# Filter network moved from the gate and up loop into the first down projection, buffers at multiples of 128 bytes, one weight ring instead of two

## The chip, the core and the metric

The kernel runs on one core of a Trainium2 chip. The metric is the device time of one execution in microseconds. A core has TensorE (PE, with its weight loads shown apart as PEld), VectorE (DVE), ScalarE (ACT), GpSimd (POOL) and SyncE (SP, which here only issues DMAs). Each has a queue of its own, worked off in order, and they meet at semaphores.

## The reference

One layer of an encoder trunk on x of 512 positions by 1024 channels, in float32:

```
x = x + 1/2 * SwiGLU_1(RMSNorm(x))            # 1024 -> 2816 -> 1024
h = RMSNorm(x); p = h @ W_in                  # -> q | k | v | x0 | x1 | v, 512 each
a = differential attention (4 heads, relative bias)
y = Hyena: short conv of width 3, long two-sided convolution, gates
x = x + concat([a, y]) @ W_out
x = x + 1/2 * SwiGLU_2(RMSNorm(x))
final RMSNorm
```

The long convolution's filters come from a small network on a position code z of 512 rows and 33 columns, which depends on no activation:

```
a = sin(freq * (z @ w1 + b1))                 # 33 -> 64
a = sin(freq * (a @ w2 + b2))                 # 64 -> 64
a = sin(freq * (a @ w3 + b3))                 # 64 -> 64
h = (a @ w4) * decay                          # 64 -> 2 x 512
```

## The kernel before

Activations lie with channels on the partitions and the 512 positions along the free axis, so each matmul is 128 x 128 weights against 128 x 512 activations. For float32 accuracy every operand is split into a high part (float32r) and the rest: each product of blocks is three matmuls, high by high, high by low, low by high (lines 1147, 1148, 1149).

Weights come in tiles of up to 8 blocks (0.5 MB), numbered through the kernel: 44 for gate and up of the first feed-forward layer (`N_FF1`), 24 for its down projection (`N_DOWN1`, in three chunks of 8, 8 and 6 blocks for each of 8 output blocks), 24 for the input projection (`N_MIX`), 8 for the output projection, and 44 and 24 again. For each tile SP loads it into one of four `raw` slots (line 282), waiting until the tile four before it has been split; ACT casts it to the high part (line 455), waiting until PE has used the tile two before it; DVE subtracts (line 723); PE runs 24 (or 18) matmuls. High and low parts have two halves in turn, in `w_hi` and `w_lo`, or for the down projection in `down_hi` and `down_lo`, which share their place with the DFT tables:

```
def ring(n):
    n = n if n < N_FF2 else n - N_FF2
    return (down_hi, down_lo) if N_DOWN1 < n <= N_MIX else (w_hi, w_lo)
```

In a pass of `gate_up` PE does a gate tile and an up tile, twice; DVE scales both sums by `rinv` (lines 810, 815), ACT takes Silu (line 498), DVE multiplies (line 820), ACT and DVE split the product into `h_hi` and `h_lo` (lines 502, 823). In a block j of `down` PE sums 22 blocks into bank 4 or 5, DVE adds half of it to the residual (`resid_add`, line 738), ACT squares it and makes `x_hi` (`resid_block`, lines 462 and 464), DVE makes `x_lo` (line 758). PE goes on to the next block in the other bank meanwhile.

The filter network is laid into passes 1 to 4 of the first gate and up loop. `mlp(k)` on PE (line 1195) is one float32 matmul, shown as two; `mlp_argument(k)` on DVE adds the bias, multiplies by the frequency and brings the argument into the range of Sin in seven instructions (lines 769 to 787); `mlp_sin(k)` on ACT takes Sin (line 474). PE's `mlp(k)` waits for `mlp_sin(k - 1)`. The result `act3` is read by the filters' matmuls at the start of the mixer stage (line 1312). The four DFT tables (0.5 MB each) are loaded by SP behind the sixth load of the input projection (lines 310 to 314).

`place` gives a buffer the next multiple of 32 bytes. The base and most sizes are multiples of 128; `rinv`, `ssq` and `lam_in` start 32 bytes past one, and `x0c`, `vx`, `vx_nat` and `q_hi` 96 bytes past one.

Of the kernel before, what the change touches and what calls it, by code (L numbers as in the profile page):

```python
# [14 lines left out]
P = 128  # L15
# [19 lines left out]
SPLIT = 2  # L35

# [39 lines left out]
def build(nc, a, out):  # L76
    ctx = ExitStack()
    with ctx:
# [5 lines left out]
        base = (nc.sbuf_base - SLAB * 4 + 31) // 32 * 32  # L84
# [23 lines left out]
        lam_in, _ = place("lam_in", [P, 4, DK])  # L108
# [5 lines left out]
        k_hi, _ = place("k_hi", [P, S], F32R)  # L114

        act3, _ = place("act3", [FO, S])
# [4 lines left out]
        cos_t, tables_at = place("cos_t", [P, NT, FQ])  # L121
        sin_t, _ = place("sin_t", [P, NT, FQ])
        cos_i, _ = place("cos_i", [P, 2, S])
        sin_i, _ = place("sin_i", [P, 2, S])
# [49 lines left out]
        z_t, _ = place("z_t", [EMB, S], at=late_at)  # L174
        w1, _ = place("w1", [EMB, FO], at=late_at + 4 * S)
        w2, _ = place("w2", [FO, FO], at=late_at + 4 * (S + FO))
        act_a, _ = place("act_a", [FO, 2, S], at=late_at + 4 * 2 * S)
        w3, _ = place("w3", [FO, FO], at=late_at + 4 * 4 * S)
# [77 lines left out]
        def ring(n):  # L256

            n = n if n < N_FF2 else n - N_FF2
            return (down_hi, down_lo) if N_DOWN1 < n <= N_MIX else (w_hi, w_lo)

# [14 lines left out]
        def _(sp):  # L275
# [8 lines left out]
            def others():  # L284

                sp.dma_start(z_t[:], a["c_z"]).then_inc(mlp_landed, 16)
                sp.dma_start(w1[:], a["hy_f_w1"][0]).then_inc(mlp_landed, 16)
                with nc.allow_non_contiguous_dma(reason="columns of constants"):
                    for k, name in enumerate(("hy_f_b1", "hy_f_b2", "hy_f_b3", "hy_f_freq")):
                        sp.dma_start(mlp_c[:, k:k + 1], a[name].rearrange("o f -> f o")).then_inc(mlp_landed, 16)  # L290
                    sp.dma_start(w2[:], a["hy_f_w2"][0]).then_inc(mlp_landed, 16)
                    sp.dma_start(w3[:], a["hy_f_w3"][0]).then_inc(mlp_landed, 16)
# [60 lines left out]
            gate_up(a["ffn1_w_gate"][0], a["ffn1_w_up"][0], N_FF1)  # L353
            down(a["ffn1_w_down"][0], N_DOWN1)
            w = a["w_in"][0].rearrange("(k p) f -> p k f", p=P)
            for h in range(HEADS):
                for m in range(6):
                    load(w[:, :, m * D_ATT + h * P:m * D_ATT + (h + 1) * P], KD, N_MIX + 6 * h + m)
                if h == 0:
                    dft_tables()  # L360
# [84 lines left out]
        def _(act):  # L445
# [5 lines left out]
            def split(kb, n0, stride=0, i=0):  # L451
                slot, half = n0 % RAW, n0 % SPLIT
                act.wait_ge(raw_landed[slot], number(16 * (n0 // RAW + 1), 16 * stride // RAW, i))
                wait(act, w_used, number(n0 - SPLIT + 1, stride, i))
                nc.scalar.copy(ring(n0)[0][:, half, 0:kb, :], raw[:, slot, 0:kb, :]).then_inc(w_hi_made, 1)  # L455
# [16 lines left out]
            def mlp_sin(k):  # L472
                act.wait_ge(mlp_arg, k + 1)
                nc.scalar.activation(act3[:] if k == 2 else act_a[:, k, :], mlp_u[:], ACT.Sin).then_inc(mlp_act, 1)


            def gate_up(ffn, n_first, i, first=False, other=None):
                for b in range(2):
# [6 lines left out]
                    if other and b == 0:  # L485
                        other()
# [17 lines left out]
            def down(s, i, last=False):  # L504
# [204 lines left out]
        def _(dve):  # L709
# [9 lines left out]
            def split(kb, n0, stride=0, i=0):  # L719
                slot, half = n0 % RAW, n0 % SPLIT  # L720
                dve.wait_ge(w_hi_made, number(n0 + 1, stride, i))
                hi, lo = ring(n0)
                nc.vector.tensor_tensor(lo[:, half, 0:kb, :], raw[:, slot, 0:kb, :],  # L723
                                        hi[:, half, 0:kb, :].bitcast(F32), ALU.subtract).then_inc(w_split, 1)
# [66 lines left out]
            def gate_up(ffn, n_first, i, first=False, other=()):  # L791

                other = list(other) + [lambda: None] * 4
                for b in range(2):
# [18 lines left out]
                    other[2 * b]()  # L813
# [11 lines left out]
                    other[2 * b + 1]()  # L825

            def down(s, i, last=False):
# [26 lines left out]
            for i in range(4):  # L854
                gate_up(0, N_FF1, i, first=i == 0, other=mlp_argument(i - 1) if i else ())
# [10 lines left out]
            with dve.Fori(0, 2) as i:  # L866
                down(1, i)
# [269 lines left out]
        def _(pe):  # L1137

            def tile(dst, operand, n0, stride=0, i=0, first=True, last=True, ready=None, between=None):
# [3 lines left out]
                hi_w, lo_w = ring(number(n0, stride, i) if isinstance(i, int) else n0)  # L1143
                for k, (hi, lo) in enumerate(operand):
                    if ready:
                        pe.wait_ge(ready[0], ready[1] + k + 1)
                    nc.tensor.matmul(dst, hi_w[:, half, k, :], hi, start=first and k == 0, stop=False)  # L1147
                    nc.tensor.matmul(dst, hi_w[:, half, k, :], lo, start=False, stop=False)  # L1148
                    ins = nc.tensor.matmul(dst, lo_w[:, half, k, :], hi, start=False, stop=last and k == kb - 1)  # L1149
# [12 lines left out]
            def gate_up(ffn, n_first, i, first=False, other=None):  # L1162
                for b in range(2):
# [15 lines left out]
                    if other and b == 0:  # L1179
                        other()  # L1180

            def down(s, i, first=False):
                for j in range(4):
                    wait(pe, resid_set, number(KD * (s - 1) + j - 1, 4, i))
# [5 lines left out]
            def mlp(k):  # L1190
                src = (z_t[:], act_a[:, 0, :], act_a[:, 1, :])[k]
# [51 lines left out]
            for i in range(4):  # L1243
                gate_up(0, N_FF1, i, first=i == 0, other=(lambda: mlp(i - 1)) if i else None)
# [7 lines left out]
            down(1, 0, first=True)  # L1252
# [316 lines left out]
```

## Time and profile before

| | us |
|---|---|
| median of 3 runs | 1064.8 |
| lowest and highest | 1063.46 and 1067.45 |
| the profiled execution, its own time | 1066.42 |
| its span, first to last instruction | 1064.6 |
| PE busy | 1037.0 (97%) |
| DVE busy | 568.4 (53%) |
| ACT busy | 334.7 (31%) |
| POOL busy | 60.8 (6%) |
| a 0.5 MB load of gate or up weights, issue to landing, median | 3.7 |

The times of rows come from that one profiled execution and are counted from the start of its span. Busy time of PE overlaps: a matmul of 512 columns is shown as 0.39 us, and in the dense stream the next one starts 0.23 us after it. The mean granted clock of TensorE is 0.987 of full speed.

### The profile page before, as it was taken

To read this page: it belongs to the slowest core of one execution; us is meant where nothing else is said; L and a number is where in the kernel's file an instruction comes from. 1 tells how busy PE (TensorE), PEld (TensorE's weight loads), DVE (VectorE), ACT (ScalarE), POOL (GpSimd) and SP (SyncE) were. 2 spreads that over 40 slices of the span, in tenths; PEclk is the share of its full clock that TensorE was granted. 3 is DMA by queue.
4 is the path that set the end of the run, shared out by engine and by line. 5 is a ranking of instruction groups with operands and counts; after the bars stand their busy time and mean duration, and the time that the engine had idled before them with its cause. 6 is when DMAs were issued, how large, how long until landed. Compare 5 with 4: busy or idle time off the path is not lost. (4 is left out here: it accounts for less than half of the span.)

```text
span 1064.6 us, 12059 instructions
## 1 busy us (share of the span) xinstructions
PE 1037.0 (97%) x4551; PEld 821.8 (77%) x4551; DVE 568.4 (53%) x722; ACT 334.7 (31%) x477; POOL 60.8 (6%) x57
## 2 busy tenths in 40 slices
PE   8999999999999999999999969999999999999996
PEld 7777788888888876777775558878888888888885
DVE  5556554544333358686857595764444445433332
ACT  6222222222232233444444203442222222222222
POOL 0000000000000010000000070310000000000000
PEclk9999999999999998999999989999999999999999
DMA  7523323333333373222221000323333332332322
GB/s 220 95 84 94 99 83 100 93 99 94 100 98 91 92 242 90 76 80 80 77 79 40 1 20 20 91 88 99 99 99 99 95 100 82 96 105 90 94 70 79
DMA packets 184460, 96.69 MB, mean 91 GB/s; under 512 B 14811, under 2 KB 181859, under 8 KB 184424
## 3 DMA queue, kind: packets, MB, share of 16 engines
q1 hardware_dynamic: 183160, 92.70, 30.0%
q0 software_dynamic: 352, 1.85, 0.6%
q10 hardware_dynamic: 912, 1.64, 0.5%
q8 instruction: 24, 0.39, 0.2%
q14 instruction: 12, 0.10, 0.0%
HBM read 94.07 MB, written 2.11 MB: 90 GB/s over the span
## 5 line engine op out<-in xcount | busy, mean ns | idle before, releaser
L1147 PE MATMUL bank<-x_hi,w_hi 128*128 128x512 f32 x872 | 345.5, 396 | 3.3 <-DVE w_lo L723 2.9
L1149 PE MATMUL bank<-x_hi,w_lo 128*128 128x512 f32 x872 | 340.5, 391 | 0.0
L1148 PE MATMUL bank<-x_lo,w_hi 128*128 128x512 f32 x872 | 340.4, 390 | 0.0
L723 DVE TENSOR_TENSOR w_lo<-raw,w_hi 128x1024 fp32r<-128x1024 f32 x121 | 148.0, 1223 | 110.6 <-ACT w_hi L455 106.2
L1147 PEld LDWEIGHTS bank<-x_hi,w_hi 128*128 128x128 f32 x872 | 164.3, 188 | 49.9 <-issue 10.1
L1149 PEld LDWEIGHTS bank<-x_hi,w_lo 128*128 128x128 f32 x872 | 164.3, 188 | 34.7
L1148 PEld LDWEIGHTS bank<-x_lo,w_hi 128*128 128x128 f32 x872 | 164.4, 189 | 34.3 <-issue 1.0
L455 ACT CAST w_hi<-raw 128x1024 fp32r<-128x1024 f32 x121 | 126.6, 1046 | 52.3 <-PE bank L1451 32.1
L1147 PE MATMUL bank<-h_hi,down_hi 128*128 128x512 f32 x336 | 130.7, 389 | 0.0
L1148 PE MATMUL bank<-h_lo,down_hi 128*128 128x512 f32 x336 | 130.7, 389 | 0.0
L1149 PE MATMUL bank<-h_hi,down_lo 128*128 128x512 f32 x336 | 130.7, 389 | 0.0
L723 DVE TENSOR_TENSOR down_lo<-raw,down_hi 128x1024 fp32r<-128x1024 f32 (+1 forms) x47 | 55.5, 1182 | 110.5 <-ACT down_hi L455 110.2
L502 ACT CAST h_hi<-bank 128x512 f32 (+1 forms) x44 | 25.8, 587 | 207.5 <-DVE bank L820 207.5
L455 ACT CAST down_hi<-raw 128x1024 fp32r<-128x1024 f32 (+1 forms) x47 | 45.8, 974 | 112.2 <-PE bank L1149 112.2
L1148 PEld LDWEIGHTS bank<-h_lo,down_hi 128*128 128x128 f32 x336 | 63.1, 188 | 13.2
L1147 PEld LDWEIGHTS bank<-h_hi,down_hi 128*128 128x128 f32 x336 | 63.1, 188 | 13.0
L1149 PEld LDWEIGHTS bank<-h_hi,down_lo 128*128 128x128 f32 x336 | 63.1, 188 | 13.0
L395 POOL TENSOR_TENSOR ssq<-ssq,sq 128x512 f32<-128x512 f32 x24 | 32.4, 1352 | 651.0 <-ACT sq L462 650.7
L498 ACT ACTIVATE silu<-bank 128x512 f32<-128x512 f32 x44 | 26.3, 599 | 132.2 <-DVE bank L810 132.2
L815 DVE TENSOR_TENSOR bank<-bank,rinv 128x512 f32<-128x512 f32 x44 | 30.7, 699 | 67.9 <-PE bank L1149 67.8
L810 DVE TENSOR_TENSOR bank<-bank,rinv 128x512 f32<-128x512 f32 x44 | 30.7, 698 | 39.2 <-PE bank L1149 39.2
L823 DVE TENSOR_TENSOR h_lo<-bank,h_hi 128x512 f32 (+1 forms) x44 | 30.4, 691 | 36.0 <-ACT h_hi L502 36.0
(222 smaller groups left out, 866.6 us busy)
## 6 DMA issues: line engine op xcount, KB each, us to landing
raw<-in_ffn_w_gate SPq DMA_DIRECT2D x44, 512.0 KB, 3.7
raw<-in_ffn_w_up SPq DMA_DIRECT2D x44, 512.0 KB, 3.7
raw<-in_ffn_w_down SPq DMA_DIRECT2D x32, 512.0 KB, 3.4
raw<-in_w_in SPq DMA_DIRECT2D x24, 512.0 KB, 3.8
raw<-in_ffn_w_down SPq DMA_DIRECT2D x16, 384.0 KB, 3.0
raw<-in_w_out SPq DMA_DIRECT2D x8, 512.0 KB, 3.4
x_nat<-in_x SPq DMA_DIRECT2D x4, 512.0 KB, 7.0
out<-o_nat SPq DMA_DIRECT2D x8, 256.0 KB, 2.9
```

Of the source, the lines that this page charges most:

```text
L395: nc.gpsimd.tensor_tensor(ssq[:], ssq[:], sq[:, b, :], ALU.add).then_inc(ssq_added, 1)
L455: nc.scalar.copy(ring(n0)[0][:, half, 0:kb, :], raw[:, slot, 0:kb, :]).then_inc(w_hi_made, 1)
L498: nc.scalar.activation(silu[:, b, :], bank[b][:], ACT.Silu).then_inc(gate_act, 1)
L502: nc.scalar.copy(h_hi[:, number(b, 2, i), :], bank[2 + b][:]).then_inc(h_hi_made, 1)
L723: nc.vector.tensor_tensor(lo[:, half, 0:kb, :], raw[:, slot, 0:kb, :], hi[:, half, 0:kb, :].bitcast(F32), ALU.subtract).then_inc(w_split, 1)
L810: nc.vector.tensor_tensor(bank[b][:], bank[b][:], rinv[:], ALU.mult).then_inc(gate_scaled, 1)
L815: nc.vector.tensor_tensor(bank[2 + b][:], bank[2 + b][:], rinv[:], ALU.mult).then_inc(up_scaled, 1)
L823: nc.vector.tensor_tensor(h_lo[:, at, :], bank[2 + b][:], h_hi[:, at, :].bitcast(F32), ALU.subtract).then_inc(h_split, 1)
L1147: nc.tensor.matmul(dst, hi_w[:, half, k, :], hi, start=first and k == 0, stop=False)
L1148: nc.tensor.matmul(dst, hi_w[:, half, k, :], lo, start=False, stop=False)
L1149: ins = nc.tensor.matmul(dst, lo_w[:, half, k, :], hi, start=False, stop=last and k == kb - 1)
```

## The change

The three steps of the filter network leave the gate and up loop and go into blocks 1, 2 and 3 of the first down projection: `mlp(j - 1)` ahead of block j on PE, the parts of `mlp_argument(j - 1)` behind the three splits of block j on DVE, and `mlp_sin(j - 1)` behind `resid_block(j)` on ACT. The loops of ACT and DVE over the down projection's halves become straight code, and ACT's loop over the gate passes begins at 1 instead of 5. Sin writes `act3` each time. The separate ring goes: all tiles use `w_hi` and `w_lo`, and the DFT tables have a place to themselves and are loaded with the small constants at the start. The network's input z lies in the place of `k_hi`, and its weights w1 to w3 in that of `lam_in`, loaded behind the first layer's gate and up weights. Buffers of 512 bytes and more begin at multiples of 128 bytes.

```diff
-                at = top[0]
-                top[0] += (size + 31) // 32 * 32
+                line = LINE if size >= 512 else 32
+                at = (top[0] + line - 1) // line * line
+                top[0] = at + size
...
-        down_lo, _ = place("down_lo", [P, SPLIT, 8, P], F32R, at=tables_at)
-        down_hi, _ = place("down_hi", [P, SPLIT, 8, P], F32R, at=tables_at + 4 * SPLIT * 8 * P)
...
+        z_t, _ = place("z_t", [EMB, S], at=k_hi_at)
+        w1, _ = place("w1", [EMB, FO], at=lam_in_at)
+        w2, _ = place("w2", [FO, FO], at=lam_in_at + 4 * FO)
+        w3, _ = place("w3", [FO, FO], at=lam_in_at + 8 * FO)
...
-            def dft_tables():
-
-                sp.wait_ge(w_used, N_MIX + 1)
                 sp.dma_start(cos_t[:], a["c_cos"].rearrange("(t p) f -> p t f", p=P)).then_inc(dft_landed, 16)
...
+            def mlp_weights():
+
+                sp.wait_ge(lam_dot, 2)
+                for dst, name in ((w1, "hy_f_w1"), (w2, "hy_f_w2"), (w3, "hy_f_w3")):
+                    sp.dma_start(dst[:], a[name][0]).then_inc(mlp_landed, 16)
...
             gate_up(a["ffn1_w_gate"][0], a["ffn1_w_up"][0], N_FF1)
+            mlp_weights()
             down(a["ffn1_w_down"][0], N_DOWN1)
...
+            def down(s, i, last=False, sines=False):
                 for j in range(4):
                     for c in range(3):
                         if not (last and j == 3 and c == 2):
                             split(CHUNKS[(c + 1) % 3][1], N_STAGE[s] + 3 * j + c + 1, 12, i)
                     resid_block(s, j, 4, i)
+                    if sines and j:
+                        mlp_sin(j - 1)
...
-            for i in range(5):
-                gate_up(0, N_FF1, i, first=i == 0, other=(lambda: mlp_sin(i - 2)) if i > 1 else None)
-            with act.Fori(5, NF // 2) as i:
+            gate_up(0, N_FF1, 0, first=True)
+            with act.Fori(1, NF // 2) as i:
                 gate_up(0, N_FF1, i)
             act.wait_ge(cols_landed, 16 * 10)
-            with act.Fori(0, 2) as i:
-                down(1, i)
+            down(1, 0, sines=True)
+            down(1, 1)
...
+            def down(s, i, last=False, arguments=False):
                 for j in range(4):
                     for c in range(3):
                         if not (last and j == 3 and c == 2):
                             split(CHUNKS[(c + 1) % 3][1], N_STAGE[s] + 3 * j + c + 1, 12, i)
+                        if arguments and j:
+                            for part in mlp_argument(j - 1)[(0, 1, 2)[c]:(1, 2, 4)[c]]:
+                                part()
                     resid_add(s, j, 4, i)
...
-            with dve.Fori(0, 2) as i:
-                down(1, i)
+            down(1, 0, arguments=True)
+            down(1, 1)
...
-                hi_w, lo_w = ring(number(n0, stride, i) if isinstance(i, int) else n0)
...
+            def down(s, i, first=False, mlps=False):
                 for j in range(4):
+                    if mlps and j:
+                        mlp(j - 1)
                     wait(pe, resid_set, number(KD * (s - 1) + j - 1, 4, i))
...
-                gate_up(0, N_FF1, i, first=i == 0, other=(lambda: mlp(i - 1)) if i else None)
+                gate_up(0, N_FF1, i, first=i == 0)
...
-            down(1, 0, first=True)
+            down(1, 0, first=True, mlps=True)
             down(1, 1)
```

## Rows read from the trace of the kernel before

**Rows 1.** Waits, 24 to 250 us: engine, line, releaser; total us, times, longest.
```profile
PE bank L1147 <- DVE w_lo L723: 2.9, 4, 0.9
```

**Rows 2.** Timeline of PE: start, length, line, operation; in brackets the idle time before.
```profile
45.93 0.39 PE L1149 MATMUL bank<-x_hi,w_lo 128*128 128x512 f32 x1
46.25 1.07 PE L1195 MATMUL bank<-z_t,w 33*64 33x512 f32 x2
47.25 0.50 PE L1147 MATMUL bank<-x_hi,w_hi 128*128 128x512 f32 x1
...
52.61 0.39 PE L1149 MATMUL bank<-x_hi,w_lo 128*128 128x512 f32 x1
53.92 0.50 PE L1147 MATMUL bank<-x_hi,w_hi 128*128 128x512 f32 x1 [0.93 <-DVE w_lo L723]
```

**Rows 3.** Timeline of all engines at the end of block 1 of the down projection.
```profile
289.33 1.22 DVE L723 TENSOR_TENSOR down_lo<-raw,down_hi 128x1024 fp32r<-128x1024 f32 x1 [4.69 <-ACT down_hi L455]
...
291.90 0.39 PE L1149 MATMUL bank<-h_hi,down_lo 128*128 128x512 f32 x1
...
292.45 0.69 DVE L738 SCALAR_TENSOR_TENSOR resid<-bank,resid 128x512 f32 x1 [1.89 <-PE bank L1149]
...
293.26 0.63 ACT L462 ACTIVATE sq<-resid 128x512 f32 x1 [3.97 <-DVE resid L738]
...
293.80 0.71 ACT L464 ACTIVATE x_hi<-resid,cols  x1
...
294.41 1.04 ACT L455 CAST down_hi<-raw 128x1024 fp32r<-128x1024 f32 x1
```

**Rows 4.** ACT: a Sin on the timeline, and the group of Silu's table loads.
```profile
62.97 0.63 ACT L474 ACTIVATE act_a<-mlp_u 64x512 f32<-64x512 f32 x1
```
```profile
L498 ACT ACT_TABLE_LOAD x2 | 2.6, 1283 | 0.0
```

**Rows 5.** Timeline of DVE: last parts of an argument.
```profile
57.22 1.39 DVE L769 SCALAR_TENSOR_TENSOR mlp_u<-mlp_k,mlp_u 64x512 f32<-64x512 f32 x2
...
62.53 0.41 DVE L787 TENSOR_SCALAR mlp_u<-mlp_u 64x512 f32<-64x512 f32 x1
```

**Rows 6.** PE's timeline, its chain, and stretches (length, busy, granted clock, DMA share, GB/s).
```profile
393.75 5.71 PE L1312 MATMUL bank<-w,act 64*128 64x512 f32 x12
...
402.77 0.79 PE L1147 MATMUL bank<-x_hi,w_hi 128*128 128x512 f32 x1
```
```profile
616.12 0.39 PE L1451 MATMUL bank<-ma_hi,w_lo 128*128 128x512 f32 x1
```
```profile
650.67 3.51 PE bank L1342 x32
...
655.66 0.43 PE bank L1449
```
```profile
401.00:402.00 1.00, 1.00 (x3) 0.69 1.20 291
...
408.00:409.00 1.00, 1.00 (x5) 0.90 0.00 0
```
```profile
619.80:619.90 0.10, 0.00 (x0) 0.63 0.00 0
```
```profile
654.00:655.00 1.00, 1.00 (x4) 0.50 1.03 363
```

**Rows 7.** SP's and ACT's timelines, and a stretch with the tables' DMAs (last: GB/s).
```profile
41.58 0.41 SPq L282 DMA_DIRECT2D raw<-in_ffn_w_gate  x1
```
```profile
55.00 1.04 ACT L455 CAST w_hi<-raw 128x1024 fp32r<-128x1024 f32 x1
```
```profile
396.00:398.00 2.00, 1.99 (x5) 1.00 1.10 363
```

**Rows 8.** Groups by line and shape: shapes, count, busy us, mean ns, idle before.
```profile
L820 DVE TENSOR_TENSOR bank<-bank,silu 128x512 f32<-128x512 f32 x44 | 30.8, 700 | 4.5
L815 DVE TENSOR_TENSOR bank<-bank,rinv 128x512 f32<-128x512 f32 x44 | 30.7, 699 | 67.9 <-PE bank L1149 67.8
```

More of the change, by code:

```diff
@@ L35 @@
 SPLIT = 2
+LINE = 128
 N_FF1 = 0
@@ L83, in build @@
         slab = ctx.enter_context(nc.sbuf_tensor("slab", [P, SLAB], F32))
-        base = (nc.sbuf_base - SLAB * 4 + 31) // 32 * 32
+        base = (nc.sbuf_base - SLAB * 4 + 127) // 128 * 128
         top = [base]
@@ L107, in build @@
         ssq, _ = place("ssq", [P, S])
-        lam_in, _ = place("lam_in", [P, 4, DK])
+        lam_in, lam_in_at = place("lam_in", [P, 4, DK])
         lam, _ = place("lam", [P, 8])
@@ L113, in build @@
         mlp_c, _ = place("mlp_c", [FO, 4])
-        k_hi, _ = place("k_hi", [P, S], F32R)
+        k_hi, k_hi_at = place("k_hi", [P, S], F32R)
+        cos_t, _ = place("cos_t", [P, NT, FQ])
+        sin_t, _ = place("sin_t", [P, NT, FQ])
+        cos_i, _ = place("cos_i", [P, 2, S])
+        sin_i, _ = place("sin_i", [P, 2, S])
         act3, _ = place("act3", [FO, S])
@@ L173, in build @@
         late_at = hid_at + 4 * (2 * NF - 7) * S
[L174 to L178, printed above, removed]
+        z_t, _ = place("z_t", [EMB, S], at=k_hi_at)
+        w1, _ = place("w1", [EMB, FO], at=lam_in_at)
+        w2, _ = place("w2", [FO, FO], at=lam_in_at + 4 * FO)
+        w3, _ = place("w3", [FO, FO], at=lam_in_at + 8 * FO)
         rel, _ = place("rel", [BUCKETS, HEADS], at=late_at + 4 * (4 * S + FO))
@@ L254, in number @@
             return n0 + i * stride if stride else n0
-        def ring(n):
-            n = n if n < N_FF2 else n - N_FF2
-            return (down_hi, down_lo) if N_DOWN1 < n <= N_MIX else (w_hi, w_lo)
         def col(name, k=0):
@@ L454, in split @@
                 wait(act, w_used, number(n0 - SPLIT + 1, stride, i))
-                nc.scalar.copy(ring(n0)[0][:, half, 0:kb, :], raw[:, slot, 0:kb, :]).then_inc(w_hi_made, 1)
+                nc.scalar.copy(w_hi[:, half, 0:kb, :], raw[:, slot, 0:kb, :]).then_inc(w_hi_made, 1)
             def resid_block(s, j, stride=0, i=0):
@@ L473, in mlp_sin, with gate_up @@
                 act.wait_ge(mlp_arg, k + 1)
-                nc.scalar.activation(act3[:] if k == 2 else act_a[:, k, :], mlp_u[:], ACT.Sin).then_inc(mlp_act, 1)
-            def gate_up(ffn, n_first, i, first=False, other=None):
+                nc.scalar.activation(act3[:], mlp_u[:], ACT.Sin).then_inc(mlp_act, 1)
+            def gate_up(ffn, n_first, i, first=False):
                 for b in range(2):
@@ L484, in gate_up @@
                         split(8, n + 1, 4, i)
-                    if other and b == 0:
-                        other()
                     if head:
@@ L502, in gate_up @@
                     nc.scalar.copy(h_hi[:, number(b, 2, i), :], bank[2 + b][:]).then_inc(h_hi_made, 1)
-            def down(s, i, last=False):
+            def down(s, i, last=False, sines=False):
                 for j in range(4):
@@ L721, in split @@
                 dve.wait_ge(w_hi_made, number(n0 + 1, stride, i))
-                hi, lo = ring(n0)
-                nc.vector.tensor_tensor(lo[:, half, 0:kb, :], raw[:, slot, 0:kb, :],
-                                        hi[:, half, 0:kb, :].bitcast(F32), ALU.subtract).then_inc(w_split, 1)
+                nc.vector.tensor_tensor(w_lo[:, half, 0:kb, :], raw[:, slot, 0:kb, :],
+                                        w_hi[:, half, 0:kb, :].bitcast(F32), ALU.subtract).then_inc(w_split, 1)
             def resid_add(s, j, stride=0, i=0):
@@ L788, in mlp_argument, with gate_up @@
                 return argument, turns, rest, clamp
-            def gate_up(ffn, n_first, i, first=False, other=()):
-                other = list(other) + [lambda: None] * 4
+            def gate_up(ffn, n_first, i, first=False):
                 for b in range(2):
@@ L812, in gate_up @@
                         split(8, n + 2, 4, i)
-                    other[2 * b]()
                     dve.wait_ge(w_used, number(n + 2, 4, i))
@@ L824, in gate_up @@
                                             ALU.subtract).then_inc(h_split, 1)
-                    other[2 * b + 1]()
-            def down(s, i, last=False):
+            def down(s, i, last=False, arguments=False):
                 for j in range(4):
@@ L854, in _ @@
             for i in range(4):
-                gate_up(0, N_FF1, i, first=i == 0, other=mlp_argument(i - 1) if i else ())
+                gate_up(0, N_FF1, i, first=i == 0)
             for k in range(2):
@@ L1146, in tile @@
                         pe.wait_ge(ready[0], ready[1] + k + 1)
-                    nc.tensor.matmul(dst, hi_w[:, half, k, :], hi, start=first and k == 0, stop=False)
-                    nc.tensor.matmul(dst, hi_w[:, half, k, :], lo, start=False, stop=False)
-                    ins = nc.tensor.matmul(dst, lo_w[:, half, k, :], hi, start=False, stop=last and k == kb - 1)
+                    nc.tensor.matmul(dst, w_hi[:, half, k, :], hi, start=first and k == 0, stop=False)
+                    nc.tensor.matmul(dst, w_hi[:, half, k, :], lo, start=False, stop=False)
+                    ins = nc.tensor.matmul(dst, w_lo[:, half, k, :], hi, start=False, stop=last and k == kb - 1)
                     if between and k == kb // 2:
@@ L1160, in sum_squares, with gate_up @@
                 nc.tensor.matmul(bank[7][:], ones[:], ssq[:], start=True, stop=True).then_inc(ssq_summed, 1)
-            def gate_up(ffn, n_first, i, first=False, other=None):
+            def gate_up(ffn, n_first, i, first=False):
                 for b in range(2):
@@ L1178, in gate_up @@
                     tile(bank[2 + b][:], x_ops, n + 1, 4, i)
-                    if other and b == 0:
-                        other()
-            def down(s, i, first=False):
+            def down(s, i, first=False, mlps=False):
                 for j in range(4):
+                    if mlps and j:
+                        mlp(j - 1)
                     wait(pe, resid_set, number(KD * (s - 1) + j - 1, 4, i))
@@ L1190, in mlp @@
             def mlp(k):
-                src = (z_t[:], act_a[:, 0, :], act_a[:, 1, :])[k]
+                src = (z_t, act3, act3)[k][:]
                 if k == 0:
@@ L1243, in _ @@
             for i in range(4):
-                gate_up(0, N_FF1, i, first=i == 0, other=(lambda: mlp(i - 1)) if i else None)
+                gate_up(0, N_FF1, i, first=i == 0)
             pe.wait_ge(late_landed, 32)
```

9 lines of the change are left out of this document (removed).

## The prediction

> **What bounds the kernel now.** I read the list of waits for PE first, then the timelines of PE, DVE and ACT around the filter network, then the granted clock in one-microsecond stretches. PE is busy nearly the whole span, so only PE's time counts: an edit on ACT, DVE or a DMA queue has a price only where PE waits for it. In the first gate and up loop PE waits four times for a weight split, and nothing else [rows 1]. The reader should see where three of those four sit: behind the filter network. The dense stream starts a 128x512 matmul every 0.23 us; at 45.93 it is cut by mlp(0), and the stream's next start is at 47.25. A second hole follows one tile later, 52.61 to 53.92, with 0.93 us of it put down to w_lo [rows 2].
>
> **The change part by part.**
>
> *Filter network out of the gate loop.* Two costs go, three times each. The network's matmul takes 47.25 - 45.93 - 0.23 = 1.09 us from the stream, and the hole at the next tile 53.92 - 52.61 - 0.23 = 1.08 us [rows 2]. That hole is DVE's: its argument waits for mlp's matmul, the up scaling queues behind it, then silu product, h_hi and h_lo, and only then the split of the next weights. In both places the first matmul after the hole takes 0.50 us instead of 0.39 [rows 2], 0.1 us more each. That is 1.09 + 1.08 + 0.2 = 2.4 us an iteration, in three iterations **-7.2 us**.
>
> *Filter network into the first down projection.* mlp(0) stands before block j = 1 and needs only z_t and w1, loaded long before: its own 1.09 + 0.1 = 1.2 us, no wait. mlp(1) and mlp(2) are different. PE issues mlp(1) before block 2, and it waits for Sin(0); ACT issues Sin(0) behind resid_block(1), which waits for resid_add(1), which waits for the last matmul of block 1. So PE has to see block 1 end, and then wait for a chain that today lies under block 2. The rows of such a block [rows 3] give its length. With T = 291.90 the start of the block's last matmul: resid_add starts at T+0.55, the square at T+1.36, x_hi at T+1.90, and the next ACT instruction at T+2.51 (today a weight cast; in the change Sin). Sin took 0.63 us [rows 4], so act3 is there at T+3.14 and mlp(1) starts at about T+3.2. Its two passes last 1.0 us (46.25 to 47.25, rows 2) and the stream resumes near T+4.2 with the 0.1 us slow start, against T+0.23 today: 4.1 us, of which 2.9 are an idle PE. Behind PE's wait stand mlp(1) and all of block 2. Two such waits (the third Sin is awaited by nobody until the filters): 8.2. Together **+9.4 us**.
>
> Does the argument chain come later still? In the last tile of a block DVE has from 290.55 (289.33 + 1.22) to 292.45 free [rows 3], 1.90 us. Into it go two of the subtractions, 1.39 us, and the clamp, 0.41 [rows 5]. With the short waits between them it just fits; at worst resid_add comes some 0.1 us later. I take nothing. ACT's and DVE's next weight splits run during PE's stall and are not late.
>
> *Table set for Sin.* Silu's set is loaded twice in the whole kernel, once for each feed-forward layer, although Sin ran three times between Silus [rows 4]: no load was needed, and Square and Copy did not evict it either. Bounds: 0 and one load of 1.28 us. I take 0.
> The Trainium skill (ScalarE: Activation LUTs, "What ACT_TABLE_LOAD costs") prices a switch of sets at about 2.7 us, drain included. By it a switch ahead of Sin(0) would add 2.7 us once, an estimate from that page; the rows show no switch.
>
> *The clock.* A stall of 2.9 us and then 1.0 us of matmuls on 64 rows and 64 columns is 3.9 us without dense work. What did the granted clock do after such stretches? After a matmul that ended at 616.51 (616.12 + 0.39) PE idled, and the clock fell from 2.4 to 1.2 GHz at about 619.8, 3.3 us on; it also fell at 654.0, after 3.3 us of 2-column matmuls that had begun at 650.67 and kept PE busy [rows 6]. Mine is as long or longer, with a little more work in it than either, so I expect a fall at each of the two stalls. The price at the lower clock: matmuls start every 0.43 us, not 0.23 (655.66 lasts 0.43 on the chain, rows 6). After 654.0 eight matmuls ran so, 8 x 0.20 = 1.6 us. During the filters it fell at about 401.4 and rose at about 408.2, and from 402.77 on that is some 13 to 14 dense matmuls, 14 x 0.20 = 2.8 us [rows 6]. Bounds for each stall: 0 and 2.8; I take 1.6, because dense work follows at once, as it did at 654. Two: **+3.2 us**.
> The Trainium skill (TensorE: Matmul & The Clock Gate, Part 1, "What's actually happening") has half clock as the default and activity as what lifts it, so by it a stall in a dense stage costs more than its own length. This speaks against the change, and the trace agrees. Without it the sum would be +2.2 us, with it +5.4.
>
> *DFT tables moved to the start.* Four DMAs of 0.5 MB go onto SP's queue before the load of weight tile 8, and three small ones leave it. They pass no wait there. Tile 8's load was issued at 41.58; its cast began at 55.00, and would begin 2.4 us earlier without mlp(0), at 52.6 [rows 7]. When these tables moved in the mixer stage the engines carried 363 GB/s, other loads among it [rows 7], so 2.1 MB take 6 to 7 us; and with the 3.7 us that such a load takes to land (median, page) tile 8 is there at about 41.6 + 6.5 + 3.7 = 52, just at its cast; PE comes to tile 8 only two tiles' splits later, past 56. Cover: the four raw slots. If the cover goes, PE waits us for us. Bounds 0 and 3 us; I take 0. In the mixer stage the DMAs go away, but no PE wait there is for a DMA, and DVE sets the pace: 0. The three weight loads behind the gate loads wait for the lambda sums, which DVE has done before its gate loop begins, and pass SP's down loads by three issues, with four raw slots as cover: 0.
>
> *128-byte starts, one ring.* Of what PE streams in its big groups, everything already starts at multiples of 128 bytes by the order of the placements; rinv and ssq do not (32 past), nor do the last mixer buffers. DVE's product with rinv took 699 ns, and with silu, which is aligned, 700 [rows 8]: 0. The down ring had two halves like w_hi and w_lo and the same waits, so one ring waits no longer: 0. ACT's and DVE's loops that become straight code are off the path: 0.
>
> **Sum.** -7.2 + 9.4 + 3.2 = +5.4 us. The profiled execution took 1066.4 us with a span of 1064.6, 1.6 above the median of the three runs shown, 1064.8, which themselves span 4 us. Against that median: 1070.2 us.
>
> **The rivals.**
> - *Both stalls, both followed by the lower clock*, 1070.2, up to 1072.6 with 2.8 us at each: 0.45. For it: the chain is in the order of the queues, and the clock fell in less.
> - *Only one of them followed by it*, +3.8 to +5.0: 1068.6 to 1069.8; 0.20. For it: a stretch of 3.9 us is little longer than the 3.3 us after which it fell, so where the stall meets the clock may decide.
> - *The clock holds*: +2.2, 1067.0; 0.17. For it: PE idles 2.9 us, less than the 3.3 after which it fell at 619.8. Against it: the stretch of two-column matmuls. It decides where the granted clock stays 1.00 in the down stage.
> - *A table load before Sin(0)*: +1.3 on top, 1071.5; 0.06. Rows 4 speak against it.
> - *Tile 8 late*: if the tables move at half the rate above, it lands some 4 to 5 us later than I say, and PE stands 3 us at about 57 us: 1073; 0.04.
> - *The other side, the mixer's start gets faster without the tables' traffic*: the 16 filter matmuls took from 393.75 to 402.77 [rows 6], 9.0 us where 16 x 0.5 = 8.0 would do, and the clock was low after them. Were that gone, up to 1 us and the 2.8 of low clock come back; with the clock held in the down stage too that is 2.2 - 3.8 = -1.6, 1063.2. It decides only if DVE's chain of filters starts earlier, and that chain shows no DMA wait: 0.05.
> The rest, 0.03, is for what I don't see.
>
> **How the numbers follow.** The point is the first case. About 0.5% (5.3 us) is what a measurement of this kernel can tell from no change. Slower than that, above 1070.1: the first case, the table load, the late tile, less some of their lower edge: 0.51. Within: one fall, clock holds, the eased mixer, and the edge: 0.44. Faster: 0.05. The range leaves out the tails of the last rivals: 1066.0 to 1073.2, which holds the clock-holds case at its low end and two long falls at its upper; the first case alone is 1069.6 to 1072.9.
>
> **What would show it.** In the profile after: no PE wait for w_lo in iterations 1 to 3 beyond the first short one, and iterations of 21.8 us; an idle PE of about 2.9 us ahead of the second and third mlp matmul, put down to ACT's Sin, near 286 and 305 us (block 1 ends at 291.9 - 7.2 + 1.2); granted clock 0.5 after each; no new ACT_TABLE_LOAD; tile 8's cast not waiting for a DMA; the tables' four DMAs near 40 us. Wrong would be: a stall of another length (then the chain of rows 3 is not the chain), a clock at 1.00 after it, or any shift in the mixer's or the second layer's stages, where I expect none.

## The result, and the profile after

| | before | after |
|---|---|---|
| median, us | 1064.13 (4 runs, 1062.98 to 1067.45) | 1077.15 (4 runs, 1076.40 to 1079.40) |
| ratio to before | | 1.0121, 95% interval 1.0093 to 1.0149 |
| the profiled execution, its time and span | 1066.42, 1064.6 | 1077.56, 1075.8 |
| mean granted clock of that execution | 0.987 | 0.985 |

The change costs 13.0 us in the medians, 11.2 us between the two profiled spans. 1070.2 was predicted, with a range up to 1073.2: slower, as forecast, but outside the range.

First the list of waits of PE, 24 to 400 us, in the kernel after (engine, line, releaser; total us, times, longest). It answers to [rows 1].

```profile
PE bank L1184 <- ACT act L466: 5.2, 2, 2.6
PE bank L1136 <- DVE w_lo L713: 0.3, 1, 0.3
```

The waits for w_lo behind the filter network are gone; in their place stand two for Sin, 2.6 us each (the stalls, below). The timeline after, around the second network matmul `mlp(1)` (start, length, engine, line; idle time before in brackets; rows between are left out), answers to [rows 3]:

```profile
286.22 0.39 PE L1138 MATMUL bank<-h_hi,w_lo 128*128 128x512 f32 x1
286.26 0.42 DVE L777 TENSOR_SCALAR mlp_u<-mlp_u 64x512 f32<-64x512 f32 x1
286.64 0.69 DVE L728 SCALAR_TENSOR_TENSOR resid<-bank,resid 128x512 f32<-128x512 f32 x1
287.37 0.63 ACT L454 ACTIVATE sq<-resid 128x512 f32<-128x512 f32 x1 [3.79 <-DVE resid L728]
287.90 0.71 ACT L456 ACTIVATE x_hi<-resid,cols 128x512 fp32r<-128x512 f32 x1
...
288.52 0.61 ACT L466 ACTIVATE act<-mlp_u 64x512 f32<-64x512 f32 x1
...
289.19 1.96 PE L1184 MATMUL bank<-act,w 64*64 64x512 f32 x2 [2.58 <-ACT act L466]
...
311.51 1.07 PE L1184 MATMUL bank<-act,w 64*64 64x512 f32 x2 [2.58 <-ACT act L466]
```

That is the predicted chain, link by link: last matmul of block 1, resid_add, square, x_hi, Sin, and only then PE; the last row is `mlp(2)`, with the same wait. The clamp ends at 286.68 and resid_add begins at 286.64: the argument just fits, as the prediction had it. What came behind the wait, in one-microsecond stretches (length, then busy time of PE, PEld, DVE, ACT and POOL, granted clock, DMA share, GB/s):

```profile
289.00:290.00 1.00, 0.81 (x1) 0.28 (x2) 0.97 (x1) 1.00 (x2) 0.42 (x1) 0.61 0.00 0
290.00:291.00 1.00, 1.00 (x2) 0.00 (x0) 0.90 (x1) 0.07 (x1) 0.00 (x0) 0.50 0.00 0
295.00:296.00 1.00, 1.00 (x4) 0.72 (x3) 0.00 (x0) 0.00 (x0) 0.00 (x0) 0.50 0.00 0
296.00:297.00 1.00, 1.00 (x6) 0.82 (x5) 0.00 (x0) 0.00 (x0) 0.00 (x0) 0.98 0.00 0
313.00:314.00 1.00, 1.00 (x5) 0.77 (x4) 1.00 (x2) 0.00 (x0) 0.00 (x0) 0.55 0.00 0
314.00:315.00 1.00, 1.00 (x4) 0.81 (x3) 0.78 (x2) 0.00 (x0) 0.00 (x0) 0.50 0.07 23
316.00:317.00 1.00, 1.00 (x5) 0.80 (x4) 0.00 (x0) 0.00 (x0) 0.00 (x0) 0.74 0.27 80
```

TensorE went from 2.4 to 1.2 GHz at both stalls. After the first it stayed there from 289.2 to 296.0, the whole `mlp(1)` (1.96 us instead of 1.07) and some eleven dense matmuls; after the second, where `mlp(2)` had still run at full rate from 311.51, from 313.1 to 316.5, some eight dense matmuls.

None of this explains the size. To find the rest, take the same instruction in both traces (of DVE, and for the output projection of PE), kernel after minus kernel before, along the whole span:

| start of the instruction | after minus before, us |
|---|---|
| the gate loop's beginning, end of passes 1, 2, 3, end of the loop | -0.4, -2.8, -5.2, -7.7, -7.7 |
| resid_add of blocks 0, 1, 2, 3 of the first down projection | -7.4, -5.8, +1.6, +7.3 |
| of blocks 4, 5, 6, 7 | +7.7, +8.1, +8.4, +8.8 |
| first `q_t` of the mixer stage, second `q_t` and later | +9.0, +7.0 |
| output projection, PE on `mh_hi`: first matmul, last | +6.9, +7.6 |
| last instruction of the second layer's gate loop | +7.6 |
| resid_add of blocks 0 to 7 of the second down projection | +8.1, 8.5, 9.0, 9.4, 9.8, 10.3, 10.7, 11.2 |

The steps at blocks 2 and 3 are the stalls. The last row has nothing of the filter network in it, and yet each block is 0.44 us longer. So something runs slower throughout the down projections, and in the output projection too. On the timeline of PE, kernel after, in the second down projection, where PE waits for nothing:

```profile
1014.88 0.39 PE L1137 MATMUL bank<-h_lo,w_hi 128*128 128x512 f32 x1
1015.11 0.40 PE L1138 MATMUL bank<-h_hi,w_lo 128*128 128x512 f32 x1
1015.34 0.39 PE L1136 MATMUL bank<-h_hi,w_hi 128*128 128x512 f32 x1
1015.57 0.40 PE L1137 MATMUL bank<-h_lo,w_hi 128*128 128x512 f32 x1
1015.81 0.39 PE L1138 MATMUL bank<-h_hi,w_lo 128*128 128x512 f32 x1
1016.04 0.40 PE L1136 MATMUL bank<-h_hi,w_hi 128*128 128x512 f32 x1
```

and in the kernel before:

```profile
1000.09 0.39 PE L1147 MATMUL bank<-h_hi,down_hi 128*128 128x512 f32 x1
1000.32 0.39 PE L1148 MATMUL bank<-h_lo,down_hi 128*128 128x512 f32 x1
1000.55 0.39 PE L1149 MATMUL bank<-h_hi,down_lo 128*128 128x512 f32 x1
1000.77 0.39 PE L1147 MATMUL bank<-h_hi,down_hi 128*128 128x512 f32 x1
```

From one `h_hi,w_hi` to the next, a *triple* of matmuls, it takes 0.70 us after (1015.34 to 1016.04) and 0.68 before (1000.09 to 1000.77). Over all recorded pairs of neighbours in the second down projection (175 in each kernel) the means are 0.700 and 0.680. The two layers have 2 x 176 such triples: 352 x 0.02 = 7.0 us. In the gate loops and the input projection the triple is 0.68 in both kernels. In the output projection it is not: where PE streams `mh_hi` and `mh_lo`, which lie in h's place by then, it is 0.70 after and 0.68 before, and its part of the same loss is 0.7 us:

```profile
696.73 0.39 PE L1438 MATMUL bank<-mh_hi,w_hi 128*128 128x512 f32 x1
...
697.43 0.40 PE L1438 MATMUL bank<-mh_hi,w_hi 128*128 128x512 f32 x1
```

```profile
687.08 0.39 PE L1449 MATMUL bank<-mh_hi,w_hi 128*128 128x512 f32 x1
...
687.76 0.39 PE L1449 MATMUL bank<-mh_hi,w_hi 128*128 128x512 f32 x1
```

In the two stretches of the down projection the clock is 1.00, the instructions and their order are the same, and PE waits for nothing. A row's own length (0.39 or 0.40) hardly shows it; only starts, three apart, do.

### The profile page after: what moved, and what is told of

Its sections match the earlier page's. It is cut to its first block and busy times, and to the rows that moved or that the text cites. A ratio compares the mean times of both kernels' runs of the same rounds, so it can differ in the third digit from the quotient of the medians.

```text
span 1075.8 us, 11999 instructions
## 1 busy us (share of the span) xinstructions
PE 1045.6 (97%) x4551; PEld 823.2 (77%) x4551; DVE 570.3 (53%) x722; ACT 335.0 (31%) x477; POOL 60.7 (6%) x57
## 5 line engine op out<-in xcount | busy, mean ns | idle before, releaser
L713 DVE TENSOR_TENSOR w_lo<-raw,w_hi 128x1024 fp32r<-128x1024 f32 x168 | 203.7, 1213 | 236.6 <-ACT w_hi L447 232.0
L447 ACT CAST w_hi<-raw 128x1024 fp32r<-128x1024 f32 x168 | 172.3, 1026 | 183.8 <-PE bank L1138 146.5
L1136 PE MATMUL bank<-h_hi,w_hi 128*128 128x512 f32 x352 | 141.0, 400 | 0.0
L1137 PE MATMUL bank<-h_lo,w_hi 128*128 128x512 f32 x352 | 140.4, 399 | 0.0
L1138 PE MATMUL bank<-h_hi,w_lo 128*128 128x512 f32 x352 | 140.4, 399 | 0.0
L1136 PEld LDWEIGHTS bank<-h_hi,w_hi 128*128 128x128 f32 x352 | 67.1, 191 | 19.2 <-issue 3.2
L1138 PEld LDWEIGHTS bank<-h_hi,w_lo 128*128 128x128 f32 x352 | 67.1, 191 | 16.2
L1137 PEld LDWEIGHTS bank<-h_lo,w_hi 128*128 128x128 f32 x352 | 67.2, 191 | 16.0
L454 ACT ACTIVATE sq<-resid 128x512 f32<-128x512 f32 x24 | 15.1, 630 | 78.4 <-DVE resid L728 66.8
L808 DVE TENSOR_TENSOR bank<-bank,silu 128x512 f32<-128x512 f32 x44 | 30.8, 700 | 4.5
```

The lines of the kernel that those rows point to most:

```text
L447: nc.scalar.copy(w_hi[:, half, 0:kb, :], raw[:, slot, 0:kb, :]).then_inc(w_hi_made, 1)
L713: nc.vector.tensor_tensor(w_lo[:, half, 0:kb, :], raw[:, slot, 0:kb, :], w_hi[:, half, 0:kb, :].bitcast(F32), ALU.subtract).then_inc(w_spl ...
L808: nc.vector.tensor_tensor(bank[2 + b][:], bank[2 + b][:], silu[:, b, :], ALU.mult).then_inc(h_made, 1)
L1136: nc.tensor.matmul(dst, w_hi[:, half, k, :], hi, start=first and k == 0, stop=False)
L1137: nc.tensor.matmul(dst, w_hi[:, half, k, :], lo, start=False, stop=False)
L1138: ins = nc.tensor.matmul(dst, w_lo[:, half, k, :], hi, start=False, stop=last and k == kb - 1)
```

## The experiments

What differs between the two dense streams is where the operands lie. `place` in the change moves `h_hi` from byte 138624 to 138752 of a partition and `h_lo` from 183680 to 183808. The first of each pair is 128 past a multiple of 256, the second is on one. `w_hi` (82048) and `w_lo` (90240) lie 128 past a multiple of 256 in both kernels, and so do `x_hi` and `x_lo`, and `down_hi` and `down_lo` in the kernel before. So my theory became: the stream is slow when the activations and the weights start at different places modulo 256. Its rivals: the single ring, `h` on a multiple of 256 by itself, the DFT tables' new place, or something of the profile alone. "Past" below always means past a multiple of 256 bytes.

### h_plus128: the kernel after, h moved by 128 bytes

```diff
+        top[0] += 128
         hid_at = top[0]
```

> The changed kernel with h_hi and h_lo 128 bytes further on (138880 and 183936 instead of 138752 and 183808), nothing else. In the changed kernel three matmuls of one block take 0.70 us in both down projections, 0.68 in every other stage. Placement theory (the start of h decides the rate of the stream): 0.68 in both down projections, 16 blocks x 0.43 = 6.9 us less than the changed kernel, about 1070 us. Ring theory (down weights in w_hi and w_lo cost the time): 0.70 stays, about 1077.

Measured: 1071.39 us (7 runs, 1068.04 to 1071.65) beside 1064.94 of before (16 runs), ratio 1.0047, interval 1.0031 to 1.0064; the kernel after stood at 1.0121. One line of placement gives back 5.8 us in the medians, 6.6 with each median taken against the kernel before of its own series. The same stretch of PE's timeline:

```profile
1015.04 0.39 PE L1137 MATMUL bank<-h_hi,w_hi 128*128 128x512 f32 x1
...
1015.73 0.39 PE L1137 MATMUL bank<-h_hi,w_hi 128*128 128x512 f32 x1
...
1016.40 0.39 PE L1137 MATMUL bank<-h_hi,w_hi 128*128 128x512 f32 x1
```

A triple is 0.68 again (1.36 for two). The end of the second down projection, 11.15 us behind before in the kernel after, is 2.7 us behind here. Both waits for Sin are as in the kernel after; the clock fell only at the second:

```profile
289.53 1.07 PE L1185 MATMUL bank<-act,w 64*64 64x512 f32 x2 [2.60 <-ACT act L467]
290.53 0.50 PE L1137 MATMUL bank<-h_hi,w_hi 128*128 128x512 f32 x1
...
308.38 1.55 PE L1185 MATMUL bank<-act,w 64*64 64x512 f32 x2 [2.60 <-ACT act L467]
```

```profile
290.00:291.00 1.00, 1.00 (x4) 0.43 (x3) 0.87 (x2) 0.42 (x1) 0.00 (x0) 1.00 0.00 0
309.00:310.00 1.00, 1.00 (x3) 0.14 (x1) 0.95 (x2) 0.26 (x1) 0.00 (x0) 0.50 0.00 0
```

This run prices the parts of a stall apart. Without a fall a stall costs 3.9 us (resid_add stands at -5.44 in block 1 and -1.55 in block 2 against before), with one 5.5 (-1.55 to +3.93).

### before_one_ring: the kernel before, its second ring gone

```diff
-            n = n if n < N_FF2 else n - N_FF2
-            return (down_hi, down_lo) if N_DOWN1 < n <= N_MIX else (w_hi, w_lo)
+            return (w_hi, w_lo)
```

> The kernel before with all weight tiles in w_hi and w_lo; the down ring's place stays unused, every address stays. Ring theory: 0.70 us for three matmuls in both down projections, about 1071. Placement theory: 0.68, within 1 us of the kernel before, about 1064.

Measured: 1065.87 us (10 runs), ratio 1.0001, interval 0.9988 to 1.0014; triple 0.680. The single ring costs nothing that this measurement can tell from 0, and is not what slows the stream.

### before_h_plus128: the kernel before, h moved by 128 bytes

```diff
+        top[0] += 128
         hid_at = top[0]
```

> The kernel before, down ring kept, with h_hi and h_lo (and the mixer buffers that share their place) 128 bytes further on, at 138752 and 183808 as in the changed kernel. Placement theory: 0.70 us for three matmuls in both down projections, about 1071. Ring theory: 0.68, about 1064.

Measured: 1073.75 us (4 runs), ratio 1.0074, interval 1.0047 to 1.0100; the triple in both down projections 0.700. The same line that mends the kernel after harms the kernel before, since here it takes h from 128 past to 0 past. Two rings, the old place of the tables, the filter network in the gate loop: none of that prevents it. The mixer's buffers in h's place move along, and `mh_hi`'s triple is 0.697 here too. The predicted 352 x 0.02 = 7.0 us lies in the interval of 5.0 to 10.7 us.

### w_plus384: the kernel after, the weights moved instead

```diff
         raw, _ = place("raw", [P, RAW, 8, P])
+        cols, _ = place("cols", [P, NCOLS])
+        top[0] = (top[0] + 127) // 128 * 128
         w_hi, _ = place("w_hi", [P, SPLIT, 8, P], F32R)
```

(`cols` leaves its old place.) Weights are now 0 past, like h; x stays 128 past.

> The changed kernel with cols placed ahead of w_hi, so that w_hi and w_lo start 384 bytes further on, at 0 past a multiple of 256 where they were 128 past one; x_hi, x_lo and h stay. If the start of h alone counts: down 0.70, gate and up 0.68, about 1077. If it is the pair of activations and weights: down 0.68 (both at 0 past 256) and gate, up and input projection 0.70 (x is 128 past, weights 0): 110 tiles x 24 x 0.0065 = 17 us more and 7 less, about 1087. Ring theory: as the changed kernel.

Measured: 1083.82 us (4 runs), ratio 1.0165, interval 1.0145 to 1.0185. The down triple is 0.680 with h still 0 past, and the gate, up and input projection's triple has become 0.70 (0.697 to 0.700 by stage). So it is neither h's place nor the weights' alone, but the two together: what one edit mends in the down projections, it breaks in the larger part of the kernel. The time is 3 us under the 1087 that was expected. Part of that is in the trace: the output projection, left out of the sum, gains 0.7 us here (0.70 back to 0.68), and the first gate loop and the input projection stayed at 0.697 and 0.698.

### w32_h64, w64_h128, w96_h192: other distances

Single executions, for the stream's rate alone, on before_one_ring: the weights start 32, 64 or 96 bytes further on, h twice as far, x stays. One of the three, the others alike:

```diff
+        top[0] += 64
         w_hi, _ = place("w_hi", [P, SPLIT, 8, P], F32R)
...
+        top[0] += 64
         hid_at = top[0]
```

> before_one_ring with weights 32 bytes and h 64 bytes further on: x starts 32 bytes less than w, h 32 bytes more, counted modulo 256. If only equality modulo 256 is fast: 0.70 us for three matmuls everywhere. If a difference below 128 costs nothing: 0.68 everywhere. If the cost grows with the distance: between, or less than 0.68 somewhere.

> before_one_ring with weights 64 bytes and h 128 bytes further on: x starts 64 bytes less than w, h 64 bytes more, modulo 256. Same alternatives: 0.70 everywhere (only equality is fast), 0.68 everywhere (a difference below 128 costs nothing), or between.

> before_one_ring with weights 96 bytes and h 192 bytes further on: x starts 96 bytes less than w, h 96 bytes more, modulo 256. From the two such runs before: 0.70 us where x stands below w by 32 and 64, 0.70 and 0.687 where h stands above by 32 and 64. Only equality is fast: about 0.70 for both. No theory has less than 0.68.

Measured: 1090.96, 1084.10 and 1091.15 us. The mean triple by the distance (activations minus weights, modulo 256), from these runs and those above:

| distance | triple, us | run and stream |
|---|---|---|
| 0 | 0.680 | kernel before, gate and down; w_plus384, down |
| +128 | 0.700 | kernel after, down; w_plus384, gate |
| -32, +32 | 0.700, 0.700 | w32_h64, gate and down |
| -64, +64 | 0.700, 0.687 | w64_h128, gate and down |
| -96, +96 | 0.703, 0.700 | w96_h192, gate and down |

Only equal starts gave 0.680. None of the distances of 32, 64 and 96 bytes is as good. Each of them was measured with one pair of starts only, so the table doesn't show that the distance alone decides; for 0 (both at 128, both at 0) and for 128 (0 against 128, either way round) there are two.

### h_lo_plus128 and w_lo_plus384: one operand of the pair

```diff
         h_hi, _ = place("h_hi", [P, NF, S], F32R)
+        top[0] += 128
         h_lo, _ = place("h_lo", [P, NF, S], F32R)
```

> The changed kernel with only h_lo 128 bytes on: h_hi starts at 0, h_lo at 128 past a multiple of 256, both weights at 128. If each matmul pays for its own pair of activations and the weights that lie in or go into the array with it: high by low (the one that streams h_lo) starts the next one after 0.227 us, the other two after 0.233; three take 0.693. If one bad operand spoils all three: 0.70; if the pair is decided by the high parts: 0.70; by the low parts: 0.68.

> The changed kernel with cols ahead of w_lo, so that w_lo starts at 0 past a multiple of 256 and w_hi stays at 128; x at 128, h at 0. While x_lo or h_lo streams, the array loads w_lo for the next matmul; while the two others stream it loads w_hi. If the weights that are loaded during the stream count: in the down stage high by low is fast (0.227) and the others slow, three in 0.693; in the gate loop high by low is slow, three in 0.687. If the weights already in the array count: the same sums, but the fast one of down and the slow one of the gate loop is the matmul with w_lo itself.

(The second puts `cols` ahead of `w_lo` alone.) If each matmul had its own price by its own pair of operands, the down triple of h_lo_plus128 (two matmuls of three unequal) would be 0.693, and in w_lo_plus384 the gate triple (one of three) 0.687 and the down triple (two of three) 0.693. Measured: 0.687, and 0.693 and 0.700; the times were 1077.16 and 1088.35 us. That simple form of the theory is refuted. A price set by neighbours too (which weights load while which activations stream) would be a candidate; no run separates it, and what the hardware does inside stays open. That all four equal is fast, and anything else measured is slower, stands.

### net_in_gate: placement, ring and tables of the change, without moving the network

The kernel before with one ring, the new `place`, the DFT tables in a place of their own and loaded at the start, and h 128 past; `mlp`, its arguments and Sin stay in the gate loop.

```diff
-                at = top[0]
-                top[0] += (size + 31) // 32 * 32
+                line = LINE if size >= 512 else 32
+                at = (top[0] + line - 1) // line * line
+                top[0] = at + size
...
+        top[0] += 128
         hid_at = top[0]
...
-                if h == 0:
-                    dft_tables()
```

> The whole change but the filter network's move, with h 128 bytes on: one ring, 128-byte starts, DFT tables loaded at the start; the network stays in the gate loop. If tables, ring and the other starts cost and give nothing: the kernel before, 1065 within 2 us. If the early tables delay weight tile 8 or ease the mixer stage: up to 3 us more or 4 us less.

Measured: 1065.81 us (10 runs) beside 1066.25 of before (19 runs), ratio 0.9991, interval 0.9974 to 1.0007. PE's wait for w_lo is that of [rows 1], four times, 2.9 us in all. The prediction's zeros for the ring, the tables and the other starts hold within this interval, as long as h stays 128 past.

### sin_early: the kernel after, mended

With h as in h_plus128, Sin goes ahead of the residual's square and x_hi on ACT, and the parts of the argument into the block's first two tiles on DVE:

```diff
-                    resid_block(s, j, 4, i)
                     if sines and j:
                         mlp_sin(j - 1)
+                    resid_block(s, j, 4, i)
...
-                            for part in mlp_argument(j - 1)[(0, 1, 2)[c]:(1, 2, 4)[c]]:
+                            for part in mlp_argument(j - 1)[(0, 2, 4)[c]:(2, 4, 4)[c]]:
```

> h_plus128 with Sin(j-1) issued ahead of resid_block(j) instead of behind it, and DVE's argument done in the first two tiles of a block instead of all three. Theory of the step (PE waits for the chain resid_add, square, x_hi, Sin, 2.6 us twice, and one of two stalls brought the lower clock): no wait of mlp for ACT, granted clock 1.00 in the down stage, so h_plus128 less 2 x 2.9 and less some 1.6: about 1061 us, 3.6 below the kernel before (three matmuls of the network at 1.2 us stay, three holes at 1.2 us go). Rival (the stall has another cause, such as the network's place in the stage): the waits stay, about 1068.

Measured: 1061.54 us (10 runs, 1059.39 to 1064.48) beside 1066.25 of before (19 runs), ratio 0.9966, interval 0.9951 to 0.9982. It beats both kernels. PE's timeline where the first stall was:

```profile
286.01 0.39 PE L1139 MATMUL bank<-h_hi,w_lo 128*128 128x512 f32 x1
...
286.33 1.07 PE L1185 MATMUL bank<-act,w 64*64 64x512 f32 x2
...
287.33 0.50 PE L1137 MATMUL bank<-h_hi,w_hi 128*128 128x512 f32 x1
```

```profile
287.00:288.00 1.00, 1.00 (x4) 0.59 (x4) 0.13 (x1) 0.84 (x2) 0.05 (x1) 1.00 0.82 246
```

No wait, no fall, and a step of 1.2 us at each `mlp` (resid_add at -7.2, -6.0, -4.8, -3.5 in blocks 0 to 3): moving the network is worth 7.2 - 3 x 1.2 = 3.6 us if nobody waits. The network's small matmuls are still there, so they alone did not bring the lower clock; in these runs it fell there only where the wait stood ahead of them.

## Why the prediction came out as it did

**The step that failed** is "128-byte starts, one ring": "Of what PE streams in its big groups, everything already starts at multiples of 128 bytes ...: 0". The premise is true and the conclusion is not. I looked at whether each start was a multiple of 128 and priced only DVE's products by it [rows 8]; what counts here is how h's start stands to the weights' modulo 256, and the change shifted h by 128. Measured: 7.0 us by the triples, 6.8 by the shifts (0.37 to 0.44 us a block, 3.3 us in the first down projection and 3.5 in the second), and 0.7 more in the output projection. It was given neither a bound nor a rival, so the range could not hold it. h_plus128 and before_h_plus128 show the cause from both sides, w_plus384 shows that it is the weights' start against h's and not h's alone, before_one_ring and net_in_gate clear the ring, the tables and the rest. Why the chip streams more slowly so, no run shows.
The Trainium skill (SBUF — State Buffer, "Operand start alignment") gives the starts that an operand may have, and says that this is about legality, not speed; the rates above are this case's own.

**The other terms**, in the profiled executions:

| term | predicted | measured | from |
|---|---|---|---|
| ahead of the gate loop | 0 | -0.4 | shift at its beginning |
| network out of the gate loop | -7.2 | -7.3 | shift from -0.4 to -7.7 |
| mlp(0) in down | +1.2 | +1.1 | -7.4 to -5.8, less 0.4 of triples |
| two stalls | +8.2 | +7.8 | 3.9 each in h_plus128 |
| clock after them | +3.2 | +4.5 | (7.4 - 3.9 - 0.4) + (5.8 - 3.9 - 0.4) |
| triples, both down projections | 0 | +6.8 | 3.3 + 3.5 by the shifts |
| triples, output projection | 0 | +0.7 | +6.9 to +7.6 |
| mixer stage | 0 | -2.0 | +9.0 to +7.0 |
| sum | +5.4 | +11.2 | spans: 1075.8 - 1064.6 |

The -0.4 us at the start has no run of its own and stays open. Two things made the total look better than it was. The wait was 0.4 us too long in the forecast and the clock 1.3 us too cheap, which partly cancel; and the -2.0 us of the mixer stage, which nothing in the prediction's sum stands for, hides 2 us of the miss. The prediction also named, as a sign of being wrong, any shift in the mixer's or the second layer's stages, and that sign came: 0.7 us in the output projection, 3.5 in the second down projection. (Its "first case alone", up to 1072.9, doesn't follow from its own 1072.6 for two long falls; the range isn't touched by it.)

*The stalls.* The links are those of the prediction, each a little shorter: with T = 286.22, resid_add at T+0.42, the square at T+1.15, x_hi at T+1.68, Sin at T+2.30, PE at T+2.97, where 0.55, 1.36, 1.90, 2.51 and 3.2 were forecast.

*The clock.* It fell after both stalls in the kernel after, in w_plus384 and in h_lo_plus128, after one of the two in h_plus128 and in w_lo_plus384. The rival with one fall was a fair one. The price varies more than I had it: 3.0 us at the first stall of the kernel after, where the 64-row matmuls themselves ran at 1.2 GHz and some eleven dense ones, 1.4 at the second with some eight, and 1.6, the forecast figure, at the one in h_plus128.

*The mixer stage* I take for no effect of the change, which is not shown. In the kernel before the clock fell during the filters [rows 6]; in the profiled execution after it did not:

```profile
401.00:402.00 1.00, 1.00 (x7) 0.81 (x6) 0.90 (x4) 0.00 (x0) 0.00 (x0) 1.00 1.07 317
```

```profile
402.76 5.71 PE L1301 MATMUL bank<-w,act 64*128 64x512 f32 x12
409.20 1.99 PE L1301 MATMUL bank<-w,act 64*128 64x512 f32 x4 [0.73 <-DVE prob L889]
411.12 0.50 PE L1136 MATMUL bank<-x_hi,w_hi 128*128 128x512 f32 x1
412.85 0.39 PE L1137 MATMUL bank<-x_lo,w_hi 128*128 128x512 f32 x1
```

The filters take 8.36 us here (402.76 to 411.12), 9.02 in [rows 6], with the same 0.73 of waiting inside, and the matmuls behind them start at full rate. Of the seven traces with the network in the gate loop it fell there in all seven, of the six with the network in the down projection in three (h_plus128, w_plus384 and h_lo_plus128, and not in after, w_lo_plus384 and sin_early). So the stalls don't decide it: h_plus128 and w_plus384 have them as the kernel after has, and there it fell. But that the moved network makes the fall rarer, these traces can't rule out. The early tables, by which the prediction's last rival had the mixer's start gain up to 3.8 us, are not enough for it: net_in_gate has them, and there it fell. And one kernel alone has both: of 16 executions of before in one series, the seven with a mean clock of 0.990 took 1063.05 to 1064.80 us, the nine with 0.986 to 0.988 took 1064.69 to 1067.01. That fits a fall which comes in some executions and not in others, 2 us apiece; only one execution of each kernel has a trace, so it is argued, not shown. It also accounts for the medians differing by 13.0 us and the profiled spans by 11.2: the profiled execution of before was one of its longer ones (1066.42 against 1064.13).
The Trainium skill (TensorE: Matmul & The Clock Gate, Part 1, "What's actually happening") says that one kernel's count of slow matmuls at its start differs from run to run. No run here counts them over several executions; the spread of the mean clock in these 16 goes the same way.

*The zeros that held.* No table load ahead of Sin: Silu's row has its two loads as in [rows 4], and Sin at 288.52 follows squares and casts with no load since Silu's. That Square did not evict the set, [rows 4] could not say, since no Square lay between there; this trace does. The tables went out where expected and weight tile 8 came in time:

```profile
L488 ACT ACT_TABLE_LOAD x2 | 2.6, 1283 | 0.0
```

```profile
38.91 0.43 SPq L298 DMA_DIRECT2D cos_t<-in_c_cos  x1
...
41.64 0.39 SPq L276 DMA_DIRECT2D raw<-in_ffn_w_gate  x1
```

```profile
52.64 1.04 ACT L447 CAST w_hi<-raw 128x1024 fp32r<-128x1024 f32 x1
```

Tile 8's load is issued at 41.64, as before [rows 7], and its cast begins at 52.64 with no wait for a DMA; predicted was 52.6.

## What to carry to other kernels

When a change moves buffers, look at the starts of what TensorE streams against the starts of its weights before costing the move at nothing, and measure the dense stream's rate over several matmuls in each stage, before and after; compare the same instruction's start along both traces, since a slope there is a slower stream and a step is a stall. A small filler matmul laid between the blocks of a dense stage is cheap (1.2 us) when its input was ready a block earlier and costs three to six times that (3.8 and 3.9 us where the clock held, 5.3 to 7.1 where it fell) when it hangs on the tail of the block just finished, behind that block's own epilogue on another engine. Place the feeding instruction ahead of the epilogue in that engine's queue.

## What the hardware showed that I had not expected

- A stream of 128x512 matmuls in which each loads its own weights started one every 0.227 us (0.680 for three) when activations and weights, high and low parts, start at the same place modulo 256 bytes, and every 0.233 us (0.700) when they are 128 apart: 3%. Distances of 32, 64 and 96 bytes, one pair of starts each, gave 0.687 to 0.703 for three.
- Buffers 256 bytes apart modulo 512 (h and the weights in before_one_ring, 0.680) are as fast as those that agree modulo 512 (h and `down_hi`, `down_lo` in the kernel before, 0.680).
- With an idle PE of 2.6 us and then matmuls on 64 rows (1.0 us at full rate) the clock fell to 1.2 GHz in eight of ten such places in five kernels (after, w_plus384, h_lo_plus128, h_plus128, w_lo_plus384), for 3.4 or 6.8 us. Where only the wait was gone and the small matmuls stayed (sin_early), it did not fall there.
